# Turning blocks of softmax weights with a diagonal of reciprocals in place of the identity, in a decoder layer on one core

## What is computed

```python
a = jax.nn.softmax(s, axis=-1).astype(v.dtype)               # fox, per head
o_fox = jnp.einsum('bhqk,bkhd->bqhd', a, v)
...
o_slc = jnp.einsum('bhgqnl,bhqnld->bqhgd', a, vsel)          # nsa, selected
o_win = jnp.einsum('bhgqk,bkhd->bqhgd', a, kwin[:, :, 1])    # nsa, window
o = jnp.stack([o_cmp, o_slc, o_win], axis=-1)
return jnp.einsum('bqhdc,bqhc->bqhd', o, gb)                 # gates
```

## Time and profile before

| | us |
|---|---|
| median of 3 runs | 1219.46 |
| lowest, highest | 1215.34, 1220.36 |
| profiled execution, its own time | 1220.0 |
| its span, first to last instruction | 1218.2 |
| TensorE busy | 1174.3 |
| VectorE busy | 536.5 |
| ScalarE busy | 419.4 |
| GpSimd busy | 147.1 |

### The profile page before, as it was taken

How to read it: one execution, slowest core, us unless ns; L and a number is a source line. 1 busy time by engine, 2 the same in 40 slices (tenths; PEclk the granted TensorE clock), 3 DMA queues, 4 the chain that set the end, 5 groups by cost and what they waited for, 6 DMA issues and landing times.

```text
span 1218.2 us, 23307 instructions
## 1 busy us (share of the span) xinstructions
PE 1174.3 (96%) x9500; PEld 1079.0 (89%) x9500; DVE 536.5 (44%) x772; ACT 419.4 (34%) x731; POOL 147.1 (12%) x151
## 2 busy tenths in 40 slices
PE   9999999999999899998989899989999999999994
PEld 6999999999999799996546557969999999999994
DVE  4433423333333653454555766564334333334334
ACT  6322312222243542224433556453232212223342
POOL 0101100001111000122202321200101000011110
PEclk9999999999999999999998999999999999999997
DMA  6322222322223133224753321122222223222221
GB/s 276 104 72 100 87 79 93 118 76 103 74 70 112 57 109 138 90 77 131 168 166 94 105 70 36 70 69 70 86 87 95 79 78 130 73 101 91 66 87 70
DMA packets 49008, 117.53 MB, mean 96 GB/s; under 512 B 8186, under 2 KB 24954, under 8 KB 43138
## 3 DMA queue, kind: packets, MB, share of 16 engines
q1 hardware_dynamic: 45746, 110.55, 27.6%
q10 hardware_dynamic: 3184, 5.88, 1.3%
HBM read 107.79 MB, written 7.97 MB: 95 GB/s over the span
## 4 chain that ended last, share of the span: by engine, by line
PE 90%; DVE 5%; issue 2%; ACT 2%; DMA 0%; DVEq 0%; SPq 0%; ACTq 0%
PE ps L1475 73%; PE ps L1898 4%; PE ps L1602 2%; PE ps L1635 2%; PE ps L1484 2%; PE ps L1619 2%; PE ps L1669 1%; DVE UT L990 1%; DVE H L994 1%; DVE row_max L1148 1%; DVE PTS L488 1%; PE ps L1568 1%; PE ps L1846 0%; DMA RAW<-in_w_gu 0%; DVE PRB L472 0%
## 5 line engine op out<-in xcount | busy, mean ns | idle before, releaser
L1475 PE MATMUL ps<-XH,WH 128*128 128x260 f32 x1776 | 363.3, 286 | 6.3 <-DVE XL L970 6.2
L1475 PE MATMUL ps<-XH,WL 128*128 128x260 f32 x1776 | 358.1, 283 | 0.0
L1475 PE MATMUL ps<-XL,WH 128*128 128x260 f32 x1776 | 357.4, 283 | 0.0
L419 ACT CAST WH<-RAW 128x1024 fp32r<-128x1024 f32 (+2 forms) x183 | 175.0, 956 | 519.7 <-PE ps L1475 500.4
L1475 PEld LDWEIGHTS ps<-XH,WH 128*128 128x128 f32 x1776 | 275.3, 189 | 11.3 <-DVE XL L970 9.1
L1475 PEld LDWEIGHTS ps<-XH,WL 128*128 128x128 f32 x1776 | 274.0, 189 | 0.0
L1475 PEld LDWEIGHTS ps<-XL,WH 128*128 128x128 f32 x1776 | 273.3, 188 | 0.0
L422 DVE TENSOR_TENSOR WL<-RAW,WH 128x1024 fp32r<-128x1024 f32 (+2 forms) x183 | 203.7, 1113 | 154.0 <-ACT WH L419 152.7
L1475 PE MATMUL ps<-UL,WH 128*128 128x260 f32 x704 | 141.9, 283 | 0.0
L1475 PE MATMUL ps<-UH,WL 128*128 128x260 f32 x704 | 141.5, 282 | 0.0
L1475 PE MATMUL ps<-UH,WH 128*128 128x260 f32 x704 | 141.3, 282 | 0.0
(11 more groups left out here) (253 smaller groups left out, 1067.3 us busy)
## 6 DMA issues: line engine op xcount, KB each, us to landing
RAW<-in_w_gu SPq DMA_DIRECT2D x44, 1024.0 KB, 4.8
RAW<-in_w_down SPq DMA_DIRECT2D x16, 768.0 KB, 4.5
RAW<-in_w_in SPq DMA_DIRECT2D x11, 1024.0 KB, 4.8
RAW<-in_w_down SPq DMA_DIRECT2D x16, 640.0 KB, 4.2
KF<-in_fox_k SPq DMA_DIRECT2D x16, 256.0 KB, 4.2
VF<-in_fox_v SPq DMA_DIRECT2D x16, 256.0 KB, 4.3
RAW<-in_w_out SPq DMA_DIRECT2D x4, 1024.0 KB, 5.8
H<-in_x SPq DMA_DIRECT2D x4, 520.0 KB, 7.0
```

Source lines behind the costliest of these rows:

```text
L419: nc.scalar.copy(WH[:, par, 0:width], RAW[:, slot, j, 0:width]).then_inc(w_hi, 1)
L1475: q = nc.tensor.matmul(ps[:, 2 * slot + half, 0:HALF], w[:, par, cols], x[:, kt0 + kt, half * HALF:(half + 1) * HALF], start=first and kt ...
```

## The change

The exponentials stay as ScalarE writes them. `divide` takes the reciprocals, multiplies them by the gates for nsa (two values per partition), and builds two 128 x 128 diagonal tiles, identity times reciprocal, with one VectorE tensor_tensor of 128 x 256. The diagonals have three slots: two in R1 (`token_rstd`, idle in this stage) and a new tile. `turn_p` becomes a matmul with the diagonal as the moving operand, so that it turns the block and scales it. `scale_p` and its two semaphores go; GpSimd's `attention` loop keeps only `follow`.

```diff
-DVE_SCALES = 2
@@
+        third_diagonal = att.put("third_diagonal", [P, 2 * P], F32)
@@
-        def scale_p(eng, tensor_scalar, u):
-
-            fox, h, br, i, _ = unit(u)
-            W = P * (i + 1)
-            eng.wait_ge(sem("att_inv"), u // 2 + 1)
-            c = 3 * h + 1 + br
-            gate, times = (None, {}) if fox else (gates[:, i, c:c + 1], {"op1": ALU.mult})
-            tensor_scalar(weights(u)[:, 0:W], weights(u)[:, 0:W], row_inv[:, u:u + 1], gate, ALU.mult,
-                          **times).then_inc(sem(scaled_by(u)), 1)
-
-        def scaled_by(u):
-            return "att_scaled_dve" if unit(u)[3] >= DVE_SCALES else "att_scaled_pool"
...
+        def diagonals(m):
+
+            n = m % 3
+            t = third_diagonal[:, :] if n == 2 else R1[:, n * 2 * P:(n + 1) * 2 * P]
+            return t.rearrange("p (j k) -> p j k", k=P)
@@ def divide(m):
                 u = 2 * m
                 dve.wait_ge(sem("att_exp"), u + 2)
-                nc.vector.reciprocal(row_inv[:, u:u + 2], row_sum[:, u:u + 2]).then_inc(sem("att_inv"), 1)
-                if unit(u)[3] >= DVE_SCALES:
-                    scale_p(dve, nc.vector.tensor_scalar, u)
-                    scale_p(dve, nc.vector.tensor_scalar, u + 1)
+                fox, h, br, i, _ = unit(u)
+                inv = row_inv[:, u:u + 2]
+                link(nc.vector.reciprocal(inv, row_sum[:, u:u + 2]))
+                if not fox:
+                    c = 3 * h + 1 + br
+                    link(nc.vector.tensor_tensor(inv, inv, view(gates[:, i, :], c, [[3, 2]]), ALU.mult))
+                if m >= 3:
+                    dve.wait_ge(sem("att_turned"), 2 * (m - 3) + 2)
+                nc.vector.tensor_tensor(diagonals(m), view(ident, 0, [[0, 2], [1, P]]),
+                                        view(inv, 0, [[1, 2], [0, P]]), ALU.mult).then_inc(sem("att_diagonal"), 1)
@@ GpSimd's attention():
                 for m in range(PAIRS):
-                    for u in (2 * m, 2 * m + 1):
-                        if unit(u)[3] < DVE_SCALES:
-                            scale_p(pool, nc.gpsimd.tensor_scalar, u)
                     follow(m)
@@ def turn_p(w):
-                pe.wait_ge(sem(scaled_by(w)), scaled_count(w))
+                pe.wait_ge(sem("att_diagonal"), w // 2 + 1)
                 if w >= 2:
                     pe.wait_ge(sem("att_odd_out" if w % 2 else "att_even_out"), w // 2)
                 for kb in range(i + 1):
-                    q = nc.tensor.transpose(ps[:, 4 + w % 2, kb * P:kb * P + P],
-                                            weights(w)[:, kb * P:kb * P + P], ident)
+                    q = nc.tensor.matmul(ps[:, 4 + w % 2, kb * P:kb * P + P], weights(w)[:, kb * P:kb * P + P],
+                                         diagonals(w // 2)[:, w % 2, :], start=True, stop=True, skip_group_check=True)
                 q.then_inc(sem("att_turned"), 1)
```

More of the change, by code:

```diff
@@ L463, in score_bank @@
             return v % 4
-        def scale_p(eng, tensor_scalar, u):
-            fox, h, br, i, _ = unit(u)
-            W = P * (i + 1)
-            eng.wait_ge(sem("att_inv"), u // 2 + 1)
-            c = 3 * h + 1 + br
-            gate, times = (None, {}) if fox else (gates[:, i, c:c + 1], {"op1": ALU.mult})
-            tensor_scalar(weights(u)[:, 0:W], weights(u)[:, 0:W], row_inv[:, u:u + 1], gate, ALU.mult,
-                          **times).then_inc(sem(scaled_by(u)), 1)
-        def scaled_by(u):
-            return "att_scaled_dve" if unit(u)[3] >= DVE_SCALES else "att_scaled_pool"
-        def scaled_count(u):
-            return sum(scaled_by(v) == scaled_by(u) for v in range(u + 1))
+        def diagonals(m):
+            n = m % 3
+            t = third_diagonal[:, :] if n == 2 else R1[:, n * 2 * P:(n + 1) * 2 * P]
+            return t.rearrange("p (j k) -> p j k", k=P)
         def turn_out(eng, copy, w, name):
```

## The result

The changed kernel took 1239.22 us (median of 4 runs, 1236.63 to 1240.85), the kernel before 1219.67 (4 runs). The ratio is 1.0158 with a 95% interval of 1.0141 to 1.0175: 19.6 us slower. 1236 was forecast, with a range of 1226 to 1248. The profiled execution of the changed kernel took 1239.66 us and spans 1237.9.

A forecast was written before the change was run, and what follows sets the result against it. TensorE, busy 96% of the span, was taken as the bound. Turning +21.7, scalings -3.6 and clock -1.7 us gave +16.4 on the profiled 1220.0; less 0.5 to the median, 1236 us, range 1226 to 1248.

The forecast's parts named there:

- The second record: TensorE's turning: a matmul leaves two records per block, 0.109 us more for each of 240 blocks, 26.2 us.
- the upper bound of 0.13: TensorE's turning: at most 0.13 us more per block if weight loads follow more slowly, 31 us for 240 blocks.
- Three quarters of it on the path: TensorE's turning: 0.75 of 28.9 us shows, +21.7 us; the rest runs while TensorE would have waited anyway.
- the slow blocks: 25 blocks turned in four half-clock stretches: the second record costs twice there, 2.7 us more, 2 us at three quarters.
- The clock: Attention stage: one half-clock stretch of 3.5 us, after a hole made by scalings, would not come, -1.7 us.
- Rival 1: Attention stage: the clock stays full and the other slow stretches vanish too, total 1227; chance 0.12.
- Scalings gone: VectorE: 5.4 us of scaling leaves the chain, gate product and diagonal add 1.8 at about three pairs, -3.6 us.
- the move to `divide`: VectorE: work moves from pairs with i = 2 and 3 to those with 0 and 1, taken at 0.
- 2 (all holes filled): Attention stage: all 16.2 us of TensorE's idle time is filled, so only +7.4 us, total 1227; chance 0.10.
- 3 (VectorE): VectorE becomes the bound: `divide` holds up copies by 14 us, half reaching TensorE, total 1243; chance 0.14.
- 4: TensorE's turning: the matmul costs what the transpose did, 0.110 us per block, total 1214, faster; chance 0.04.
- 5, the factor of four: TensorE's turning: transposes four times faster than f32 matmuls, as the skill page says, +54 us, total 1273; chance 0.03.

The follow-up runs named there:

- m_plain: Kernel before with blocks turned by a plain f32 matmul against the identity, scalings on VectorE and GpSimd kept: 1238.26 us, ratio 1.0144, +18.2 us.

## Why the prediction was right, by its steps

- **The second record, 26.2 us:** right in kind (480 records), somewhat small in size. TensorE's turning grew by 0.123 us per block, 29.6 us in all, under the upper bound of 0.13. There is also a slip in the sum: 0.217 - 0.110 is 0.107, not 0.109.
- **Three quarters of it on the path, +21.7 us with 2.0 us for the slow blocks:** without the slow blocks this is 19.7 us at full clock. The runs give 17.4 to 18.2 us with the gain of the clock in it, and 20 to 22 without. Taking the stage of both profiles and crediting the time at half clock (17.2 us by the earlier trace rows and 6.8 us by the two windows below, so up to 8.6 and 3.4 us lost), 180.5 became 203.2: +22.7; less the 0.9 to 2.2 for the diagonals that is 20.5 to 21.8. So this term was up to 2 us too small. Three quarters was a good share: 22 of 29.6. It was not even, though: nine tenths show in the steady pairs, and the guests' holes swallow more of the rest.
  The changed kernel's stretches at the lower clock:

```profile
566.20:569.60 3.40, 3.34 (x10) 1.41 (x12) 1.59 (x4) 1.03 (x5) 0.00 (x0) 0.50 0.75 183
665.20:668.60 3.40, 3.40 (x26) 2.85 (x24) 1.26 (x3) 0.00 (x0) 0.00 (x0) 0.50 0.00 0
```

- **The clock, -1.7 us, with +2.0 for the slow blocks:** about nothing was forecast, and the reason given, the end of the scalings, is not borne out. The clock took 4.1 us less at most over the four timed executions, worth 2 to 4 us, and m_plain got the same with its scalings kept. Rival 1 happened in part.
- **Scalings gone, -3.6 us:** the step that failed. Removing them is worth 3 to 4 us (4.0 with the clock in it); the prediction had 5.4. But what replaces them was booked at 1.8 us on the path "at about three pairs", and the move to `divide` at 0; together they cost 4 to 6, so that this term came out at +1 to +2. The chain of waits before could not show that: at four places among the guests VectorE's work came in time behind one reciprocal, and late behind reciprocal, gate product and diagonal. I had argued the cover from 720 to 752 us, the stretch with the fewest guests, and there it holds. The gate products beside GpSimd's instructions, 10.0 us in sum instead of 5.4, were not foreseen either.
- **The sum:** +16.4 forecast, +19.6 measured. VectorE's part was put some 5 us too low and the turning up to 2; the clock gave back 2 to 4 us that were not booked. These errors went against each other, and the near total rests partly on that luck.
- **Rivals:** 2 (all holes filled) did not happen, TensorE still waits behind guests. 3 (VectorE) happened at the guests, not as a bound, with 1 to 2 us net instead of 7. 4 fell with the 480 records. 5, the factor of four, fell too: the factor is two.

By the rule of the Trainium skill, page "Perfetto Trace Analysis", section "Transposes" (use a transpose for a logical transpose), the trace agrees: m_plain, in which nothing but that was changed, lost 18.2 us.

## What to carry to other kernels

Folding a scale into a transpose is not free on the engine that does the transposing: a 128 x 128 f32 block costs one record as a transpose and two as a matmul, 0.12 us more, and where that engine sets the pace nearly all of it shows. Before moving work off engines with idle time, take it out altogether in one run: here all scaling was worth 4.0 us, so no replacement that costs TensorE 26 could win. Small instructions in front of work that another engine waits for cost at those places even where their engine is idle for a good part of the stage (VectorE four tenths of it here, 125.31 us busy of 211). And a granted clock is judged from all timed executions; single profiles of one kernel gave 0.96 and 0.98 here.

## What the runs showed that I had not expected

- A VectorE instruction on two elements per partition took 2.29 us instead of 0.16 beside a GpSimd tensor_tensor of 2.35 us. The stall goes with GpSimd's instruction, not with the size of the victim: all six gate products that were stretched ran beside one. What it cost TensorE came ten microseconds later.
- An fp32r record of 128 columns is 0.117 us behind the last, as one of 260 columns is (0.12): half the columns brought no shorter distance here.
- The clock followed the second record: kernels with f32 matmuls lost 13.9 to 14.6 us to it (19.2 with each diagonal twice), those with transposes 17.2 to 19.6, the one with a single short fp32r matmul per block 25.3. The Trainium skill, page "TensorE: Matmul & The Clock Gate", section "Part 4: PE-mode transpose", says that the full clock does not engage for transpose mode. The gain with f32 matmuls points the way of that rule, but as a matter of the mode alone no run here shows it: pairs 5 to 15 of the kernel before were turned by transposes at full clock (the row for 560 to 600 us above), and the lowest clock came with plain matmuls.
